# Later lead for the score pass and a later shift transpose in the forgetting-attention schedule

## The chip, the core and the metric

The kernel runs on one core of a Trainium2 chip. The metric is the device time in microseconds (us) of one launch. One launch computes both layers for 2048 tokens. Engines are named as in the profile: PE (TensorE), DVE (VectorE), ACT (ScalarE), POOL (GpSimd), SP (SyncE, which only issues transfers here).

## What is computed

The reference is two layers. Each normalises its input, projects it with one matrix, runs four groups of heads, gates them, projects back and adds the input. The change touches the first group alone, the forgetting attention: four heads of width 64, softmax over all earlier tokens with a decay that is added to the scores.

```python
def _fox_attention(q, k, v, f_logit, b_f, q_norm, k_norm):
    q = _rmsnorm(q, q_norm)
    k = _rmsnorm(k, k_norm)
    log_f = jax.nn.log_sigmoid((f_logit + b_f).astype(jnp.float32))
    Ft = jnp.cumsum(log_f, axis=1).transpose(0, 2, 1)
    ...
        s = jnp.einsum("bqhd,bkhd->bhqk", qi, k, preferred_element_type=jnp.float32) * scale
        s = s + Fi[..., :, None] - Ft[:, :, None, :]
        s = jnp.where(kpos[None, :] <= qpos[:, None], s, -jnp.inf)
        p = jax.nn.softmax(s, axis=-1)
        return jnp.einsum("bhqk,bkhd->bqhd", p.astype(v.dtype), v)
```

## The kernel before

Each layer is a row of phases, and every phase ends in a barrier of all engines. Their names are prefixes in the trace: pj, rp and rs (projection, recurrence), a normalising phase, fx (the forgetting attention, `phase_fox`), and so (the window attention, the short convolution, the output projection). What is won or lost inside fx moves everything behind it by the same amount, once in each layer.

In fx the work is cut into eight blocks, R = 0 to 7: two heads at a time (blocks 0 to 3 are heads 0 and 1, blocks 4 to 7 are heads 2 and 3), and for them four stretches of 512 queries. With Q = R % 4, a block has 4Q + 4 tiles of 128 keys. The softmax needs each query's greatest score before its exponentials, so each block is passed over twice. These are its steps, with the letter that the program's list `order` gives them:

- **r** (4 pieces): queries and keys of a block are rounded and their remainders taken (ACT, DVE, POOL). Pieces 2 and 3 cost DVE two operations each (L1321, L1322).
- **s** (4, 8, 12 or 16 pieces): first pass. PE makes scores with queries in the rows (L1244, and L1246 for the mask on the diagonal) into one of two PSUM buffers `SS`; DVE takes their greatest value (L1332). PE waits with piece n until DVE has done piece n - 2.
- **x**: DVE folds the greatest values of a block into `LS` (L1340), once all its s pieces are done.
- **l**: PE transposes `LS` into PSUM `LT` (L1253), ACT copies it into the block's query operand (L1390, two copies). The block's second pass cannot begin before it.
- **v**: PE transposes a block's values into the same `LT` (L1233), DVE copies them out (L1327). l, v and u (below) share the one `LT`, and each waits until the one before has been copied.
- **m** (4, 8, 12 or 16 tiles): second pass. PE makes the scores again with keys in the rows (L1268, L1269, L1271), ACT takes their exponential (L1407), PE multiplies the tile before by the values (L1223), and the exponentials are summed by DVE (L1311 for the first, L1314) or, for odd tiles outside Q = 0, by POOL (L1203, L1205). The last four tiles of a block are the diagonal ones, 512, 384, 256 and 128 queries wide.
- **o, u**: the block's result is copied out and divided by the sums.

Every engine runs its own part of the one list `order` strictly in the list's order. `plan()` writes that list: it walks through the m tiles, and after each one takes as many pieces of r, s, x and v (the list `beside`) as a running goal asks for. Two numbers matter here. The goal jumps up shortly before the end of a block, so that all s pieces of the next block are listed by then (L1123: from the fourth tile before the end). And l is put in turn by L1102: with the next block's turn less one tile, so in front of a block's last m tile, but never over four tiles behind x.

Of the kernel before, what the change touches and what calls it, by code (L numbers as in the profile page):

```python
# [1030 lines left out]
def phase_fox(nc, l, projT, fa, consts, mixT):  # L1031
# [6 lines left out]
    with ExitStack() as ctx:  # L1038
        P = Phase(nc, ctx, f"fx{l}")
        two = range(2)  # L1040
        NQ, QT = T // TB, TB // 128
# [13 lines left out]
        nm = [P.sb(f"nm{p}", [128, 2, NT, NQ]) for p in two]  # L1055
# [15 lines left out]
        keys = [QT * Q + QT for Q in range(NQ)]  # L1071
# [4 lines left out]
        def plan():  # L1076

            beside = [("r", 0, i) for i in range(4)] + [("v", 0, 0)]
            for R in range(NR):
                n = len(stat[R % NQ])
                for i in range(n):
                    if R + 1 < NR and i >= n - 4:
                        beside.append(("r", R + 1, i - n + 4))
                    beside.append(("s", R, i))
                beside.append(("x", R, 0))
                if R + 1 < NR:  # L1090
                    beside.append(("v", R + 1, 0))
            turns, order, done, ns, nm = [], [], 0, 0, 0
            total = sum(len(stat[R % NQ]) for R in range(NR))

            def ahead(goal):
                nonlocal done, ns
                while done < len(beside) and (ns < goal or beside[done][0] == "x"):
                    order.append(beside[done])
                    ns += beside[done][0] == "s"
                    if beside[done][0] == "x":  # L1100
                        r = beside[done][1]
                        turns.append((min(nm + 4, max(nm, sum(keys[i % NQ] for i in range(r)) - 1)), ("l", r, 0)))  # L1102
                    done += 1

            def turned(now):
                while turns and turns[0][0] <= now:
                    order.append(turns.pop(0)[1])

            ahead(len(stat[0]))
            turned(1)  # L1110
            ahead(len(stat[0]) + 3)
            for R in range(NR):
                for j in range(keys[R % NQ]):
                    turned(nm)
                    order.append(("m", R, j))
                    nm += 1
                    if R > 0 and j == 0:
                        order.append(("o", R - 1, 0))
                    if R > 0 and j == 2:
                        order.append(("u", R - 1, 0))  # L1120
                    goal = len(stat[0]) + 3 + min(nm, 24) * 3 // 2 + max(0, nm - 24) * 19 // 20
                    for r in range(1, NR):
                        if nm >= sum(keys[i % NQ] for i in range(r)) - 4:  # L1123
                            goal = max(goal, sum(len(stat[i % NQ]) for i in range(r + 1)))
                    ahead(min(total, goal))
            return order + [("o", NR - 1, 0), ("u", NR - 1, 0)]

        order = plan()
        lt_n = {}
        for k, R, x in order:  # L1130
# [786 lines left out]
```

## Time and profile before

| | |
|---|---|
| median of 3 runs | 3596.78 us (3592.81 to 3598.64) |
| the profiled execution's own time | 3596.78 us |
| its span | 3595.0 us |
| PE, PEld busy | 3230.6 us (90%), 2306.3 us |
| DVE, ACT, POOL busy | 1569.9 us, 1015.5 us, 546.7 us |
| fx in the first layer | about 1259 to 1540 us |
| fx in the second layer | about 3054 to 3336 us |

The page gives shares over the whole program. The change works in about 560 us of it, so the rows below are taken from the two fx stretches and read in order of time.

### The profile page before, as it was taken

Reading aid. Unit: us, or ns where it says so; the run is one execution under the profiler, and the core shown is the slowest. Engines: PE = TensorE matmul, PEld = TensorE weight load, DVE = VectorE, ACT = ScalarE, POOL = GpSimd, SP = SyncE. Lnnn points to the kernel's source line nnn. Section 1 sums busy time; section 2 is a strip of 40 time slices with the busy share of each in tenths; the row PEclk is TensorE's granted clock in tenths of the full one; section 3 lists DMA queues with packets and bytes.
Section 4 is the critical chain, followed back from the end, with each engine's and each line's share of the span. In section 5 each row is a group of like instructions: output and inputs, shape, how many; then the busy total and the mean of one; then the engine's idle time right before and its main releaser. Section 6 shows DMA issues by size and latency. Waiting matters only on the chain. (4 is left out here: it accounts for less than half of the span.)

```text
span 3595.0 us, 62105 instructions
## 1 busy us (share of the span) xinstructions
PE 3230.6 (90%) x24644; PEld 2306.3 (64%) x24644; DVE 1569.9 (44%) x2258; ACT 1015.5 (28%) x1892; POOL 546.7 (15%) x304
## 2 busy tenths in 40 slices
PE   6979979999998879959969799799999987799599
PEld 4768867777775244437748688577777752444377
DVE  4127722222223558557541277222222234675575
ACT  4014412122222135432240144121222221354322
POOL 4101000000000023332241010000000000233322
PEclk9989989999999769979989899899999996699799
DMA  3225432222222220067332254322222222100663
GB/s 121 73 72 160 144 95 63 66 66 69 77 67 99 118 58 27 9 195 214 117 116 73 72 169 138 93 66 63 66 73 75 66 106 109 58 27 9 194 214 117
DMA packets 357722, 343.27 MB, mean 95 GB/s; under 512 B 95388, under 2 KB 290972, under 8 KB 353592
## 3 DMA queue, kind: packets, MB, share of 16 engines
q1 hardware_dynamic: 288520, 298.53, 26.3%
q10 hardware_dynamic: 68928, 40.93, 4.2%
q8 instruction: 191, 3.13, 0.4%
q14 instruction: 83, 0.68, 0.1%
HBM read 208.46 MB, written 130.91 MB: 94 GB/s over the span
## 5 line engine op out<-in xcount | busy, mean ns | idle before, releaser
L124 PE MATMUL rs_acc<-h_hi,rs_w_hi 128*128 128x512 f32 x1024 | 428.3, 418 | 0.0
L128 PE MATMUL rs_acc<-h_lo,rs_w_hi 128*128 128x512 f32 x1024 | 417.8, 408 | 0.0
L130 PE MATMUL rs_acc<-h_hi,rs_w_lo 128*128 128x512 f32 x1024 | 414.5, 405 | 0.0
L110 POOL TENSOR_TENSOR rs_w_lo<-rs_raw,rs_w_hi 128x1024 fp32r<-128x1024 f32 x32 | 76.4, 2386 | 1236.2 <-POOLq L109 1236.2
L124 PE MATMUL rp_acc<-h_hi,rp_w_hi 128*128 128x512 f32 x512 | 205.5, 401 | 40.9 <-PEq L121 40.9
L1693 PE MATMUL so_acc<-so_wo_hi,so_m_hi 128*128 128x512 f32 x512 | 209.2, 409 | 27.7 <-POOL so_m_lo L1615 24.0
L124 PEld LDWEIGHTS rs_acc<-h_hi,rs_w_hi 128*128 128x128 f32 x1024 | 192.2, 188 | 55.0 <-issue 16.5
L130 PEld LDWEIGHTS rs_acc<-h_hi,rs_w_lo 128*128 128x128 f32 x1024 | 192.6, 188 | 43.2
L1407 ACT ACTIVATE fx_prob<-fx_ST 128x512 f32<-128x512 f32 (+3 forms) x320 | 155.5, 531 | 224.1 <-PE fx_ST L1271 129.7
L128 PEld LDWEIGHTS rs_acc<-h_lo,rs_w_hi 128*128 128x128 f32 x1024 | 192.7, 188 | 36.6
L124 PE MATMUL pj_acc<-h_hi,pj_w_hi 128*128 128x512 f32 (+1 forms) x512 | 207.6, 405 | 5.3 <-PEq L121 5.3
L141 ACT COPY rs_stage<-rs_acc 128x512 f32<-128x512 f32 x128 | 75.0, 586 | 483.3 <-ACTq L140 483.3
L128 PE MATMUL rp_acc<-h_lo,rp_w_hi 128*128 128x512 f32 x512 | 207.8, 406 | 0.0
L128 PE MATMUL pj_acc<-h_lo,pj_w_hi 128*128 128x512 f32 (+1 forms) x512 | 205.1, 401 | 0.0
L130 PE MATMUL pj_acc<-h_hi,pj_w_lo 128*128 128x512 f32 (+1 forms) x512 | 205.0, 400 | 0.0
L1695 PE MATMUL so_acc<-so_wo_lo,so_m_hi 128*128 128x512 f32 x512 | 204.6, 400 | 0.0
L1694 PE MATMUL so_acc<-so_wo_hi,so_m_lo 128*128 128x512 f32 x512 | 204.2, 399 | 0.0
L130 PE MATMUL rp_acc<-h_hi,rp_w_lo 128*128 128x512 f32 x512 | 200.4, 391 | 0.0
L1332 DVE TENSOR_REDUCE fx_nm<-fx_SS 128x2 f32<-128x1024 f32 (+3 forms) x160 | 166.9, 1062 | 34.3 <-PE fx_SS L1244 20.5
L141 DVE COPY pj_stage<-pj_acc 128x512 f32<-128x512 f32 (+1 forms) x64 | 44.2, 690 | 286.9 <-DVEq L140 286.9
L1223 PE MATMUL fx_O<-fx_prob,fx_vs 128*64 128x512 f32 (+3 forms) x640 | 161.5, 586 | 0.0
L1205 POOL TENSOR_TENSOR fx_sump<-fx_sump,fx_prob 128x1024 f32<-128x1024 f32 (+2 forms) x60 | 123.1, 2051 | 248.6 <-ACT fx_prob L1407 248.6
(256 smaller groups left out, 6055.7 us busy)
## 6 DMA issues: line engine op xcount, KB each, us to landing
projT<-rs_stage SPq DMA_DIRECT2D x128, 256.0 KB, 2.1
pj_xb<-x SPq DMA_DIRECT2D x32, 512.0 KB, 3.4
projT<-rp_stage SPq DMA_DIRECT2D x64, 256.0 KB, 3.1
rs_raw<-w_in ACTq DMA_DIRECT2D x32, 512.0 KB
rs_nat<-rw SPq DMA_DIRECT2D x128, 128.0 KB, 2.4
so_stage<-x SPq DMA_DIRECT2D x64, 256.0 KB, 3.0
rp_pre<-projT SPq DMA_DIRECT2D x16, 899.5 KB, 7.6
projT<-pj_stage SPq DMA_DIRECT2D x56, 256.0 KB, 2.0
```

Source lines behind the costliest of these rows:

```text
L110: self.nc.gpsimd.tensor_tensor(self.w_lo[q][:, :, 0:m], self.raw[:, :, 0:m], self.w_hi[q][:, :, 0:m].bitcast(F32), ALU.subtract).then_inc( ...
L124: ins = M(acc, self.w_hi[q][:, k, 0:m], self.h_hi[:, k, cols], start=(k == 0), stop=False)
L128: M(acc, self.w_hi[q][:, k, 0:m], self.h_lo[:, k, cols], start=False, stop=False)
L130: ins = M(acc, self.w_lo[q][:, k, 0:m], self.h_hi[:, k, cols], start=False, stop=(k == KC - 1))
L141: copy(self.stage[e][0:m, :], self.acc[e][0:m, :]).then_inc(self.stage_rdy[e], 1)
L1205: G.tensor_tensor(sump[R % 2][:, :, lo:TB], sump[R % 2][:, :, lo:TB], prob[nt % NP][:, :, lo:TB], ALU.add).then_inc(s["add_p"], 1)
L1223: ins = M(O[64 * h:64 * h + 64, lo:TB], vs[p][:, j, 64 * h:64 * h + 64], prob[i % NP][:, h, lo:TB], start=(j == 0), stop=(j == keys[Q] - 1))
L1332: V.tensor_reduce(nm[p][:, :, t, c:c + 1], SS[ns % 2][:, :, 0:width(t, c)], AX.X, ALU.max, negate=True).then_inc(s["m_rdy"], 1)
L1407: A(prob[nt % NP][:, h, lo:TB], ST[h][:, lo:TB], ACT.Exp).then_inc(s["p_rdy"], 1)
L1693: M(a, m_hi[e][:, c, rows], wo_hi[:, c, cols], start=(i == 0), stop=False)
L1694: M(a, m_lo[e][:, c, rows], wo_hi[:, c, cols], start=False, stop=False)
L1695: ins = M(a, m_hi[e][:, c, rows], wo_lo[:, c, cols], start=False, stop=(i == KC - 1))
```

## The change

Two numbers in `plan()` change, and nothing else.

```diff
-                        turns.append((min(nm + 4, max(nm, sum(keys[i % NQ] for i in range(r)) - 1)), ("l", r, 0)))
+                        turns.append((min(nm + 4, max(nm, sum(keys[i % NQ] for i in range(r)))), ("l", r, 0)))
...
-                        if nm >= sum(keys[i % NQ] for i in range(r)) - 4:
+                        if nm >= sum(keys[i % NQ] for i in range(r)) - 2:
```

The first puts l directly in front of the next block's first tile. The second lets the goal jump two m tiles later. Each engine's instructions stay the same in number and kind; their order changes at four places of each layer: the ends of blocks 0, 1, 2 and 6. At the ends of blocks 3, 4 and 5 the list stays as it was.

On PE at the end of block 1 (first layer), before the change, l (L1253) stands in front of the last m tile, and v (L1233) and an s piece (L1244) stand behind that tile:

```order
L1223 MATMUL fx_O<-fx_prob,fx_vs 64x384 x2
L1253 MATMUL fx_LT<-fx_ident,fx_LS 67x128 x4
L1268 MATMUL fx_ST<-fx_qa,fx_ka 128x128
L1269 MATMUL fx_ST<-fx_qb,fx_kb 128x128
L1271 MATMUL fx_ST<-fx_identb,fx_cmb 128x128
L1268 MATMUL fx_ST<-fx_qa,fx_ka 128x128
L1269 MATMUL fx_ST<-fx_qb,fx_kb 128x128
L1271 MATMUL fx_ST<-fx_identb,fx_cmb 128x128
L1223 MATMUL fx_O<-fx_prob,fx_vs 64x256 x2
L1233 MATMUL fx_LT<-fx_ident,fx_rv 128x128 x4
L1244 MATMUL fx_SS<-fx_kb,fx_qb 128x512 x2
L1268 MATMUL fx_ST<-fx_qa,fx_ka 128x512
```

In the changed kernel, at the same place on PE, from the last m tile's end:

```order
L1271 MATMUL fx_ST<-fx_identb,fx_cmb 128x128
L1223 MATMUL fx_O<-fx_prob,fx_vs 64x256 x2
L1233 MATMUL fx_LT<-fx_ident,fx_rv 128x128 x4
L1244 MATMUL fx_SS<-fx_kb,fx_qb 128x512 x2
L1253 MATMUL fx_LT<-fx_ident,fx_LS 67x128 x4
L1268 MATMUL fx_ST<-fx_qa,fx_ka 128x512
```

So l has moved behind the tile, behind v and behind the s piece, and the first matmul of block 2 follows it directly. Blocks 0 and 2 end in the same way; at the end of block 6 there is no v and no s piece left, and l moves over the last tile alone.

On DVE at the end of block 6, the difference is one sum (L1314, a tile of 512 queries and two heads) that moves from behind x (L1340) to between the last s pieces (L1332):

```order
 L1332 TENSOR_REDUCE fx_nm<-fx_SS 128x2 x2
 L1314 TENSOR_TENSOR fx_sumd<-fx_sumd,fx_prob 128x1024
-L1332 TENSOR_REDUCE fx_nm<-fx_SS 128x2 x4
+L1332 TENSOR_REDUCE fx_nm<-fx_SS 128x2 x2
+L1314 TENSOR_TENSOR fx_sumd<-fx_sumd,fx_prob 128x1024
+L1332 TENSOR_REDUCE fx_nm<-fx_SS 128x2 x2
 L1340 TENSOR_REDUCE fx_LS<-fx_nm 128x4 x2
-L1314 TENSOR_TENSOR fx_sumd<-fx_sumd,fx_prob 128x1024
```

On PE two m tiles have come forward between the s pieces there, and with them their exponentials on ACT and this sum on DVE. At the end of block 1 DVE's order changes in the same way:

```order
 L1332 TENSOR_REDUCE fx_nm<-fx_SS 128x2
 L1314 TENSOR_TENSOR fx_sumd<-fx_sumd,fx_prob 128x1024
-L1332 TENSOR_REDUCE fx_nm<-fx_SS 128x2 x5
+L1332 TENSOR_REDUCE fx_nm<-fx_SS 128x2 x3
+L1314 TENSOR_TENSOR fx_sumd<-fx_sumd,fx_prob 128x1024
+L1332 TENSOR_REDUCE fx_nm<-fx_SS 128x2 x2
 L1321 TENSOR_TENSOR fx_qa<-fx_rq,fx_qb 64x512
```

There the sum that followed x now stands three reductions after the sum before it, and two tiles of m have come forward on PE. At the end of block 2 two tiles come forward as well, and at the end of block 0 one.

## Rows read from the trace of the kernel before

**Rows 1.** Stretches of fx, layer one: us, busy PE PEld DVE ACT POOL, clock, DMA
```profile
1259.20:1540.00 280.80, 243.22 (x1048) 122.00 (x1048) 181.56 (x190) 127.05 (x249) 87.18 (x58) 0.88 0.10 31
...
1317.80:1334.80 17.00, 15.86 (x42) 7.38 (x44) 11.77 (x15) 2.56 (x5) 3.00 (x3) 0.50 0.11 33
...
1485.00:1495.30 10.30, 9.97 (x26) 4.26 (x26) 4.11 (x6) 2.18 (x4) 1.64 (x1) 0.50 0.00 0
```

**Rows 2.** Waits of PE from 1284 to 1540 us: total, times, longest
```profile
PE fx_SS L1244 <- DVE fx_nm L1332: 11.9, 13, 3.4
```

**Rows 3.** Timeline of PE, end of block 1: start, us, instruction [idle before]
```profile
1318.62 1.82 PE L1244 MATMUL fx_SS<-fx_kb,fx_qb 66*128 66x512 f32 x3 [2.37 <-DVE fx_nm L1332]
...
1325.05 0.78 PE L1268 MATMUL fx_ST<-fx_qa,fx_ka 128*128 128x512 f32 x1
...
1329.32 0.69 PE L1268 MATMUL fx_ST<-fx_qa,fx_ka 128*128 128x384 f32 x1
...
1338.51 0.40 PE L1268 MATMUL fx_ST<-fx_qa,fx_ka 128*128 128x512 f32 x1
```

**Rows 4.** Timeline of DVE, end of block 1
```profile
1317.89 1.81 DVE L1332 TENSOR_REDUCE fx_nm<-fx_SS 128x2 f32<-128x512 f32 x2
...
1328.82 0.24 DVE L1340 TENSOR_REDUCE fx_LS<-fx_nm 128x4 f32<-128x12 f32 x2
```

**Rows 5.** Groups of DVE by shape, layer one: count, busy us, mean ns, idle
```profile
L1314 DVE TENSOR_TENSOR fx_sumd<-fx_sumd,fx_prob 128x1024 f32<-128x1024 f32 x24 | 46.0, 1916 | 13.5 <-ACT fx_prob L1407 11.7 <-issue 0.2
...
L1327 DVE COPY fx_vs<-fx_LT 128x512 f32<-128x512 f32 x8 | 5.5, 688 | 8.6 <-PE fx_LT L1233 8.4
```

**Rows 6.** Timeline of PE, end of block 0
```profile
1294.64 0.67 PE L1268 MATMUL fx_ST<-fx_qa,fx_ka 128*128 128x384 f32 x1
...
1298.48 0.58 PE L1268 MATMUL fx_ST<-fx_qa,fx_ka 128*128 128x256 f32 x1
...
1301.13 0.65 PE L1253 MATMUL fx_LT<-fx_ident,fx_LS 128*67 128x128 f32 x4
...
1303.16 0.63 PE L1233 MATMUL fx_LT<-fx_ident,fx_rv 128*128 128x128 f32 x4 [0.24 <-ACT fx_qb L1390]
...
1304.10 0.40 PE L1268 MATMUL fx_ST<-fx_qa,fx_ka 128*128 128x512 f32 x1
```

**Rows 7.** Timeline of ACT, end of block 0
```profile
1301.82 1.19 ACT L1390 ACTIVATE fx_qb<-fx_LT 3x512 fp32r<-3x512 f32 x2 [1.33 <-PE fx_LT L1253]
```

**Rows 8.** Timeline of DVE, end of block 0
```profile
1291.07 2.17 DVE L1332 TENSOR_REDUCE fx_nm<-fx_SS 128x2 f32<-128x1024 f32 x2 [0.27 <-PE fx_SS L1244]
...
1298.41 0.23 DVE L1340 TENSOR_REDUCE fx_LS<-fx_nm 128x4 f32<-128x8 f32 x2
```

**Rows 9.** Timeline of PE, end of block 2
```profile
1364.65 0.73 PE L1244 MATMUL fx_SS<-fx_kb,fx_qb 66*128 66x512 f32 x2 [0.53 <-DVE fx_nm L1332]
...
1367.65 0.48 PE L1268 MATMUL fx_ST<-fx_qa,fx_ka 128*128 128x512 f32 x1
...
1369.97 0.44 PE L1268 MATMUL fx_ST<-fx_qa,fx_ka 128*128 128x384 f32 x1
...
1378.30 0.48 PE L1268 MATMUL fx_ST<-fx_qa,fx_ka 128*128 128x512 f32 x1
```

**Rows 10.** Timeline of DVE, end of block 6
```profile
1482.94 3.47 DVE L1332 TENSOR_REDUCE fx_nm<-fx_SS 128x2 f32<-128x1024 f32 x3
```

**Rows 11.** Timeline of PE, start of block 7
```profile
1499.22 0.47 PE L1268 MATMUL fx_ST<-fx_qa,fx_ka 128*128 128x512 f32 x1 [0.76 <-ACT fx_prob L1407]
```

**Rows 12.** Stretches of fx, layer two (columns of the first group)
```profile
3161.00:3167.80 6.80, 6.66 (x16) 2.73 (x16) 6.58 (x10) 1.44 (x3) 1.24 (x3) 0.50 0.04 8
...
3280.50:3290.70 10.20, 8.71 (x23) 3.97 (x24) 6.49 (x8) 1.69 (x3) 0.00 (x0) 0.50 0.00 0
```

**Rows 13.** Timeline of PE, layer two, end of block 2
```profile
3160.01 0.73 PE L1244 MATMUL fx_SS<-fx_kb,fx_qb 66*128 66x512 f32 x2 [0.53 <-DVE fx_nm L1332]
...
3176.00 0.48 PE L1268 MATMUL fx_ST<-fx_qa,fx_ka 128*128 128x512 f32 x1
```

## Prediction, made before the changed kernel ran

> **What bounds the kernel now.** I read the page first, then the stretches of fx with their granted clock, then PE's waits inside fx, then the timelines of PE, DVE and ACT at the ends of the four blocks whose order changes. Inside fx of the first layer PE is busy 243.2 of 280.8 us [rows 1], so fx is mostly PE-bound. What is left has three causes. The first is PE standing before an s piece for DVE's reductions, 11.9 us in 13 waits once the stage is under way, the longest 3.4 us [rows 2]. The second is the granted clock: it is 0.50 (1.2 GHz) over 17.0 us from the end of block 1 on, and over 10.3 us from the end of block 6 on, each time after a wait for DVE [rows 1, 3]. The third is at the start of fx and is not touched. The changed places are the ones with the longest waits, so the change works where something can be won, but on DVE and on the clock as much as on PE.
>
> What a tile costs at the two clocks: the 512-wide diagonal tile takes 1369.97 - 1367.65 = 2.32 us at 2.4 GHz at the end of block 2 [rows 9] and 1329.32 - 1325.05 = 4.27 us at 1.2 GHz at the end of block 1 [rows 3]. A microsecond of PE-bound work at the low clock thus wastes (4.27 - 2.32) / 4.27 = 0.46 us.
>
> **The change, place by place (first layer; the start of the next block's tiles before and after).** One chain is common to all: l starts at 1301.13, ACT's two copies run from 1301.82 to 1303.01, and PE gets the release at 1303.16 [rows 6, 7]. That is 2.0 us from the start of l to what waits for its copies. Before, this lay under the last m tile, v and an s piece. Now the next block's first matmul stands right behind l, and everything on PE is queued behind that matmul. PE itself does 0.6 us of the 2.0 and idles the rest. In front of l stands v's copy on DVE (0.69 us [rows 5]), since both use `LT`.
>
> End of block 0. One tile comes forward in front of four s pieces, at a moment when PE is the late one (DVE had idled only 0.27 us for the first of them [rows 8]). The tile takes 1298.48 - 1294.64 = 3.84 us at the low clock [rows 6], and DVE's whole row of reductions and remainders, unbroken up to x, is late by that: x ends at 1298.64 + 3.84 = 1302.5. Behind x DVE has two short sums that I take at 0.96 and 0.69 by their widths (384 and 256 queries, against 0.69 for the copy of as many elements as the second), then v's copy 0.69 and 0.15 for the release: l at 1305.0, block 1 at 1307.0. It was 1304.10 [rows 6]. Cost 2.9 us. If the remainders of block 2 absorb a part of it, the cost is 1.5.
>
> End of block 1. Before, PE stood 2.37 us for DVE [rows 3]; now a tile at full clock (2.3 us) fills just that. DVE is the chain from then on. From the end of its reductions at 1319.70 to the end of x at 1329.06 [rows 4] is 9.4 us, of which 0.5 was idle that goes; one sum is inserted. The 24 sums of that size take 1.92 us in the mean [rows 5], which I take; one that has DVE alone would be near the reductions of as many elements, 3.47 / 3 = 1.16 [rows 10]. So x ends at 1319.7 + 8.9 + 1.9 = 1330.5; then a sum of 0.69, v's copy 0.69 and 0.15: l at 1332.0, block 2 at 1334.0. It was 1338.51 [rows 3], since four tiles ran behind x at half clock. Gain 4.5 us (from 3.5 to 5.3 with the sum at 2.9 or 1.16).
>
> The Trainium skill, "GPSIMD Engine Reference", section Specifications, says that GpSimd shares its SBUF interfaces with VectorE, with contention for VectorE instructions that have two SBUF inputs, which these sums are. The trace agrees in the mean of 1.92 us against 1.16 for a reduction that reads PSUM [rows 5, 10]. By a rule of no contention the term would be 5.3 instead of 4.5.
>
> End of block 2. Here PE's waits were short (0.53 us and less) and the clock was full [rows 9], so the two tiles have little to fill. The second-last reductions now wait for PE (some 1.2 us), the sum adds 1.9, so x comes some 3.1 us later; the last m tiles, already done by then, don't help. With v, the small s pieces, l and its 2.0 us I get block 3 at about 1379.0 against 1378.30 [rows 9]. Cost 0.7, from -0.8 to 2.5.
>
> End of block 6. DVE's last four reductions began at 1482.94, the sum in front of them being done [rows 10]. Now: four reductions of 1.16, one sum of 1.92, 0.1 of latency and x 0.25 make 1489.85; l at 1490.0, block 7 at 1492.05. It was 1499.22 [rows 11]. Gain 7.2 us, from 6.0 to 8.0.
>
> Per layer at an unchanged clock from there: -4.5 - 7.2 + 2.9 + 0.7 = -8.1 us. The second layer has the same stage, so -16.2 us in both.
>
> **The clock takes it back.** The new waits sit close together. At the end of block 1 PE has done all its tiles by about 1329 and stands until 1332, does l, and stands again until 1334; at the end of block 6 it stands 1.1 and 1.4 us around l; at the end of block 0 some 1.5 and 1.4; at block 2 three short ones. Before, the clock fell after a single wait of 2.37 us [rows 3], and in the second layer it fell at the end of block 2 after waits of about 0.5 [rows 13]. So I expect falls at most of these places, and now just in front of the next block's tiles, which are PE-bound. Before, block 2's and block 7's first tiles ran at the full clock. The spans of 0.50 after a fall inside the stage are 6.8, 10.2 and 10.3 us [rows 1, 12], and 17.0 where PE was not dense. I take 8.5, less about 1 us that lies under the new wait: 7.5 x 0.46 = 3.4 us each. I take three falls of the four in each layer: 10.2 us. Per layer: -8.1 + 10.2 = +2.1 us, in both +4.2.
>
> One fall goes away. In the second layer the clock was low for 6.8 us at block 2 [rows 12], which the first layer did not have; between the same two matmuls, layer two took 3176.00 - 3160.01 = 15.99 us and layer one 1378.30 - 1364.65 = 13.65 [rows 9, 13]. So that fall cost 2.3 us, which is also the lower price of a fall. With the two tiles between the s pieces PE stays dense there: -2.3. Sum: +1.9 us. The profiled execution took 3596.78 us around its span of 3595.0, and the median of the runs is the same number, so the forecast is 3598.7 us. A measurement of this kernel can tell about 0.2% (7.2 us) from no change.
>
> Costed at nothing: the loads (SP's list is the same; their releases come some us later, far ahead of use), the casts of r on ACT and POOL (both idle half of the stage [rows 1]). If a load were late, PE would show a wait for a transfer, and does not now.
>
> **The rivals.**
> A, the clock holds. The tiles that come forward keep PE dense through the old waits, and the new waits are 1 to 1.5 us each with l between them. Then -16.2 - 2.3 is 3578, and with one fall in each layer 3585. For it: waits of 0.76 us in front of block 7 and 0.53 at block 2 passed at the full clock in layer one [rows 9, 11]. Against it: the wait of 2.37 [rows 3], and the new ones sum to more than that in as short a time. Chance 0.30.
> B, slower: the wait for l's copies, placed directly before a PE-bound stretch, sends the clock down at all four places and for the longer span. Its place is the first tiles of blocks 1, 2, 3 and 7, its price (10.2 - 1) x 0.46 = 4.2 us each, 16.9 a layer against the 8.1 gained: +8.8, in both +17.6, less 2.3: 3612. It decides from an average of 1.9 us a place on. With only three long falls it is 3603. Chance 0.25 for all four.
> C, the inserted sums cost DVE up to 2.9 us each and x is late everywhere: one more us at three places of each layer, +6, 3605. For it: the mean of 1.92 already holds doubled ones. Chance 0.10.
> The forecast, small gains and falls that cancel: 0.35, its own range 3590 to 3606.
>
> **Chances and range.** Faster by over 0.2%: A, nearly whole, and a little of the forecast, 0.31. Slower by over 0.2% (above 3604): B, half of C and a little of the forecast, 0.32. Within: 0.37. The range goes to the inner part of A and of B, 3582 to 3613.
>
> **What would show it.** In the profile after: PE's 2.37 and 3.4 us waits for the reductions at the ends of blocks 1 and 6 gone; one wait of 1 to 1.5 us on L1268 for ACT's copies L1390 in front of blocks 1, 2, 3 and 7, and none before; block 7's first tile about 9 us behind the start of the last four reductions instead of 16.3 [rows 10, 11]; fx_LT L1253 waiting for DVE (the copy of v, or x). And the granted clock: 0.50 just behind these waits if the forecast or B holds, 1.00 there if A does. The prediction is wrong if the clock stays up at three or more of the places, if block 0 does not start block 1 later, or if the time in fx changes by more than 9 us in a layer.

## The result and the profile after

The changed kernel takes 3625.73 us in the median of 6 runs (3617.81 to 3633.53), the kernel before 3597.71 us (6 runs, 3591.26 to 3603.74). The ratio is 1.0078 with a 95% interval of 1.0063 to 1.0093: 28 us slower. The forecast was 3598.7 and its range ended at 3613, so the prediction was wrong. The profiled execution has a span of 3622.8 us (before 3595.0) at a mean granted clock of 0.921 (before 0.929). The two stages of fx grew by 16.7 and 12.0 us, 28.7 together: all of the loss is there.

The page after, busy time of each engine. PE has the same 24644 matmuls and is busy 25.3 us longer (3230.6 before), so most of the loss is slower matmuls and not idle time (25.3 of the 27.8 us by which the span grew).

```profile
PE 3255.9 (90%) x24644; PEld 2321.5 (64%) x24644; DVE 1577.3 (44%) x2258; ACT 1018.9 (28%) x1892; POOL 549.4 (15%) x304
```

Stretches of fx in layer one, to be read beside [rows 1] (the third number from the end is the granted clock): the whole stage, then the part of block 1 that runs at half clock, the tiles from there to the next fall, and the low stretches at the starts of blocks 2, 3 and 7.

```profile
1259.20:1557.00 297.80, 259.05 (x1048) 130.93 (x1048) 185.47 (x190) 127.81 (x249) 87.57 (x56) 0.82 0.10 30
1307.20:1320.30 13.10, 13.07 (x34) 6.87 (x36) 3.48 (x4) 4.18 (x7) 1.04 (x1) 0.50 0.00 1
1320.30:1333.90 13.60, 12.16 (x53) 5.73 (x49) 11.07 (x10) 7.42 (x14) 6.09 (x4) 1.00 0.06 20
1333.90:1351.00 17.10, 15.46 (x50) 8.65 (x49) 9.87 (x13) 5.48 (x11) 2.00 (x3) 0.50 0.16 47
1385.00:1402.20 17.20, 14.89 (x40) 7.58 (x42) 8.52 (x16) 6.92 (x12) 1.31 (x2) 0.50 0.15 46
1508.00:1521.70 13.70, 12.55 (x30) 5.32 (x32) 0.69 (x1) 4.89 (x9) 1.04 (x1) 0.50 0.01 1
```

All four changed places run at half clock, for 13.1 to 17.2 us each. Before, there was one such stretch of 17.0 from the end of block 1 on and one of 10.3 from the end of block 6 on [rows 1]; the low clock from the start of fx ended at 1300.7, ahead of block 1 (1304.10). Now that first low clock goes on 13.1 us into block 1, and PE is busy 13.07 of these 13.10 us, so it does dense work at half clock the whole time. In layer two the clock rises for 3.4 us near the end of block 0 and falls again for 17.1 us, of which 6.7 lie in block 1; the stretches of blocks 2, 3 and 7 there are 17.1, 17.1 and 13.7 us.

Waits of PE in layer one after the change, to be read beside [rows 2]: total, times, longest.

```profile
PE fx_SS L1244 <- DVE fx_nm L1332: 8.5, 13, 1.9
PE fx_ST L1268 <- ACTq L1392: 6.5, 4, 1.6
PE fx_LT L1253 <- DVE fx_LS L1340: 1.1, 1, 1.1
```

The waits for DVE's reductions fell from 11.9 to 8.5 us, and the longest from 3.4 to 1.9. In their place stand four waits for ACT's copies of `LT` (L1392 is the release behind L1390) and one for x (L1340). The three rows sum to 16.1 us against 11.9, but over the whole program PE's idle time grew by only 27.8 - 25.3 = 2.5 us.

Timeline of PE in layer one: the first matmul of block 1, the tile that came forward at the end of block 1, the first matmuls of blocks 2 and 3, then l and the first matmul of block 7. To be read beside [rows 3, 6, 9, 11].

```profile
1307.23 0.77 PE L1268 MATMUL fx_ST<-fx_qa,fx_ka 128*128 128x512 f32 x1 [1.62 <-ACTq L1392]
...
1325.18 0.39 PE L1268 MATMUL fx_ST<-fx_qa,fx_ka 128*128 128x512 f32 x1
...
1344.22 0.77 PE L1268 MATMUL fx_ST<-fx_qa,fx_ka 128*128 128x512 f32 x1 [1.62 <-ACTq L1392]
...
1390.73 0.77 PE L1268 MATMUL fx_ST<-fx_qa,fx_ka 128*128 128x512 f32 x1 [1.62 <-ACTq L1392]
...
1506.85 0.65 PE L1253 MATMUL fx_LT<-fx_ident,fx_LS 128*67 128x128 f32 x4 [1.06 <-DVE fx_LS L1340]
...
1509.15 0.77 PE L1268 MATMUL fx_ST<-fx_qa,fx_ka 128*128 128x512 f32 x1 [1.65 <-ACTq L1392]
```

The first matmul of blocks 2, 3 and 7 took 0.40, 0.48 and 0.47 us before and takes 0.77 now. The wait is 1.62 us at three of the places and 1.65 at the fourth.

Timeline of DVE in layer one: at the end of block 1 an inserted sum, at the end of block 2 the inserted sum, a remainder behind it and x, then the end of block 6.

```profile
1330.02 1.23 DVE L1314 TENSOR_TENSOR fx_sumd<-fx_sumd,fx_prob 128x1024 f32<-128x1024 f32 x1
...
1377.05 1.22 DVE L1314 TENSOR_TENSOR fx_sumd<-fx_sumd,fx_prob 128x1024 f32<-128x1024 f32 x1
1378.19 2.32 DVE L1321 TENSOR_TENSOR fx_qa<-fx_rq,fx_qb 64x512 fp32r<-64x512 f32 x1
...
1385.40 0.25 DVE L1340 TENSOR_REDUCE fx_LS<-fx_nm 128x4 f32<-128x16 f32 x2
...
1499.48 2.34 DVE L1332 TENSOR_REDUCE fx_nm<-fx_SS 128x2 f32<-128x1024 f32 x2
1501.92 2.26 DVE L1314 TENSOR_TENSOR fx_sumd<-fx_sumd,fx_prob 128x1024 f32<-128x1024 f32 x1
```

Two of the inserted sums took 1.23 and 1.22 us and one 2.26. The remainder behind the sum of block 2 took 2.32 us, where most others of its kind in this stage took 0.67 to 0.69.

### The profile page after: what moved, and what is told of

It is laid out like the page before. It is cut to its first block and busy times, and to the rows that moved or that the text cites. A ratio compares the mean times of both kernels' runs of the same rounds, so it can differ in the third digit from the quotient of the medians.

```text
span 3622.8 us, 62105 instructions
## 1 busy us (share of the span) xinstructions
PE 3255.9 (90%) x24644; PEld 2321.5 (64%) x24644; DVE 1577.3 (44%) x2258; ACT 1018.9 (28%) x1892; POOL 549.4 (15%) x304
## 5 line engine op out<-in xcount | busy, mean ns | idle before, releaser
L1332 DVE TENSOR_REDUCE fx_nm<-fx_SS 128x2 f32<-128x1024 f32 (+3 forms) x160 | 166.5, 1061 | 70.3 <-PE fx_SS L1244 51.5
L1223 PE MATMUL fx_O<-fx_prob,fx_vs 128*64 128x512 f32 (+3 forms) x640 | 170.7, 617 | 0.0
```

Of the source, the lines that this page charges most:

```text
L1223: ins = M(O[64 * h:64 * h + 64, lo:TB], vs[p][:, j, 64 * h:64 * h + 64], prob[i % NP][:, h, lo:TB], start=(j == 0), stop=(j == keys[Q] - 1))
L1332: V.tensor_reduce(nm[p][:, :, t, c:c + 1], SS[ns % 2][:, :, 0:width(t, c)], AX.X, ALU.max, negate=True).then_inc(s["m_rdy"], 1)
```

## The experiments

The expectations name four theories by letters. The first two ask which half of the change costs: the wait behind l (W), where the later l alone costs and the later goal gains, or the goal (G), where the later goal costs, through DVE's sums. The other two ask by what it costs: the clock (C), where the waits of the new order keep PE at 1.2 GHz and the loss goes if PE is given something to do in them, or the waits and DVE's later work themselves (D), where the clock only goes along and filling the waits changes nothing. "Before" in each comparison is the kernel before in the same session (medians 3595.2, 3597.98 and 3596.48).

**One half of the change at a time.** The later l alone (L1102) and the later goal alone (L1123):

```diff
-  turns.append((min(nm + 4, max(nm, sum(keys[i % NQ] for i in range(r)) - 1)), ("l", r, 0)))
+  turns.append((min(nm + 4, max(nm, sum(keys[i % NQ] for i in range(r)))), ("l", r, 0)))
```
```diff
-  if nm >= sum(keys[i % NQ] for i in range(r)) - 4:
+  if nm >= sum(keys[i % NQ] for i in range(r)) - 2:
```

> Theory W (the move of l alone does the harm: a wait of 1.6 us for ACT's two copies in front of blocks 1, 2, 3 and 7, and a fall of the granted clock with it): at least 20 of the 28 us of the whole change show here, 3616 to 3635 us, with four waits of L1268 for L1392 in each layer, and more low clock in fx than before. Theory G (the goal's move does it, by sums of 1.2 to 2.4 us put into DVE's row before x, and by the tile that comes forward at block 0): under 10 us over the kernel before, below 3608.

Measured: 3638.04 us, ratio 1.0111 (1.0086 to 1.0136).

> Theory W: with l where it was, the moved goal is a gain: the waits of 2.4 and 3.4 us at blocks 1 and 6 are filled, block 0 costs about 2, so 3583 to 3596 us. Theory G: most of the 28 us is here, 3615 or more, with x later at blocks 0, 1 and 2.

Measured: 3618.71 us, ratio 1.0062 (1.0044 to 1.0079). Each half costs by itself, 43 and 23 us, and both together cost 28. W asked for a gain of the later goal and G for a later l that costs under 10, so neither holds; and the 3638 us lie above W's range. The waits of PE in layer one of the later l alone:

```profile
PE fx_SS L1244 <- DVE fx_nm L1332: 10.6, 11, 3.4
PE fx_ST L1268 <- ACTq L1392: 6.8, 4, 1.9
```

And of the later goal alone, with its low stretches around the starts of blocks 2 and 3 (columns of the stretches above):

```profile
PE fx_SS L1244 <- DVE fx_nm L1332: 7.4, 11, 1.9
PE fx_LT L1253 <- DVE fx_LS L1340: 5.4, 3, 2.4
PE fx_LT L1253 <- DVE fx_vs L1327: 2.9, 1, 2.9
```
```profile
1332.20:1356.10 23.90, 21.95 (x68) 12.37 (x69) 11.54 (x15) 6.56 (x13) 2.82 (x4) 0.50 0.11 33
1386.80:1407.30 20.50, 19.37 (x58) 9.73 (x58) 8.35 (x16) 7.97 (x15) 1.76 (x2) 0.50 0.14 39
```

The later l brings the four waits for ACT and leaves the 3.4 us wait; the later goal takes that one away and makes l wait for x and v instead. Either way the clock is low for 106 to 107 us in layer one (before 61).

**Something for PE to do in the waits.** The following kernels issue extra matmuls in front of chosen instructions. They write a score buffer that the next tile overwrites, so they change no output. The list `FILL` says where and how many: `("m",1,0): 7` is 7 matmuls in front of tile 0 of block 1. The `wait_ge` holds them until that buffer is free. Here it is for the changed kernel, 48 in each layer.

```diff
+            def keep_busy(n):
+                if n:
+                    pe.wait_ge(s["p_rdy"], 2 * nt - 1)
+                for _ in range(n):
+                    M(ST[0][:], K1[0][0][:, 0:128], Q1[0][0][:, 0:TB], start=True, stop=True)
+            FILL = {("m",1,0): 7, ("m",2,0): 7, ("m",3,0): 7, ("m",7,0): 7, ("l",7,0): 4,
+                    ("s",2,10): 2, ("s",2,11): 2, ("s",4,0): 8, ("s",4,1): 3, ("s",4,2): 1}
...
+                    keep_busy(FILL.get((k, R, x), 0))   # ahead of s, l and m
```

> The changed kernel, with matmuls of no use (each 128x512, 0.23 us at 2.4 GHz) put on PE where it waits at the four places: 7 in front of the first tile of blocks 1, 2, 3 and 7, 4 in front of l of block 7, 12 among the s pieces of block 4 and 4 among those of block 2. They write a score buffer that the next tile overwrites. Theory C (most of the loss is the granted clock at 1.2 GHz behind the waits): the low stretches behind the four places vanish or shrink, and the time falls by 12 to 30 us below the changed kernel's 3625, to 3596 to 3613, though PE has more to do. Theory D (the loss is the waits and DVE's later row, the clock only goes along): the time stays, or grows by up to 10 us, since nothing waits less.

Measured: 3591.6 us, ratio 0.9989 (0.9979 to 0.9999). With 96 matmuls more than the changed kernel it is 34 us faster than it, more than theory C had expected (3596 to 3613), and D is out. Its stretches in layer one: the stage, its one low stretch behind block 0, and all behind that.

```profile
1263.20:1530.70 267.50, 248.68 (x1096) 130.31 (x1096) 181.10 (x187) 124.42 (x246) 80.70 (x52) 0.91 0.09 27
1332.00:1338.80 6.80, 5.53 (x15) 4.22 (x15) 2.35 (x3) 1.66 (x3) 0.00 (x0) 0.50 0.32 101
1338.80:1530.70 191.90, 186.28 (x861) 92.78 (x860) 132.50 (x127) 94.80 (x189) 68.55 (x40) 1.00 0.05 17
```

The same for the kernel before, filled at its own waits (s pieces of blocks 2, 3 and 7, 36 in each layer):

```diff
+            FILL = {("s",2,7): 10, ("s",2,9): 1, ("s",2,10): 1, ("s",2,11): 2,
+                    ("s",7,14): 14, ("s",7,15): 2, ("s",3,13): 2, ("s",3,14): 2, ("s",3,15): 2}
```

> The kernel before, with the same kind of matmul put under its own waits for the reductions: 14 among the s pieces 7 to 11 of block 2, 6 among s pieces 13 to 15 of block 3, 16 in front of s pieces 14 and 15 of block 7. Theory C: the low stretches of 17.1 us behind block 1 and 10.2 us behind block 6 go, and with them 0.46 us for each us that PE was dense in them, 4 to 5 and 4 us in each layer, and 2 in the second layer at block 2: 3575 to 3585 us. Theory D: no gain, 3592 to 3605.

Measured: 3575.39 us, ratio 0.9945 (0.9928 to 0.9961). So the kernel before loses up to 20 us of this kind as well (the two stages of fx show 15 of them in the profiled executions), and the clock does not hide a gain of the change: filled against filled, it still costs 16 us.

**The control.** The same number of matmuls in the kernel before, put where PE does not wait:

```diff
+            FILL = {("m",3,4): 9, ("m",3,6): 9, ("m",3,8): 9, ("m",3,10): 9}
```

> A control: the kernel before, with 9 of the matmuls of no use in front of each of the tiles 4, 6, 8 and 10 of block 3, where PE is dense and the clock full, so 36 in a layer as many as before_busy has. If the matmuls gain by something other than filled waits, this is no slower. By their own length, 72 x 0.235 us, it is 17 us slower: 3608 to 3616.

Measured: 3610.32 us, ratio 1.0033 (1.0022 to 1.0043). So 72 matmuls cost 12 us where PE is busy and bring 20 where it waits; it is their place that counts. Layer one of the control beside that of the filled kernel before:

```profile
1266.90:1544.50 277.60, 253.00 (x1084) 129.23 (x1084) 177.04 (x187) 124.62 (x246) 80.01 (x52) 0.88 0.09 26
```
```profile
1266.40:1528.40 262.00, 243.59 (x1084) 125.53 (x1084) 178.41 (x187) 124.17 (x246) 79.31 (x52) 0.92 0.09 28
```

**Which waits decide.** The changed kernel with 7 matmuls in front of the first tile of blocks 1, 2, 3 and 7 and nothing else, and then with only the others of its list:

```diff
+            FILL = {("m",1,0): 7, ("m",2,0): 7, ("m",3,0): 7, ("m",7,0): 7}
```
```diff
+            FILL = {("l",7,0): 4, ("s",2,10): 2, ("s",2,11): 2, ("s",4,0): 8, ("s",4,1): 3, ("s",4,2): 1}
```

> The changed kernel with 7 matmuls of no use in front of the first tile of blocks 1, 2, 3 and 7 alone, so only the new waits of 1.6 us are filled and not those among the s pieces and in front of l. If these four waits are what brings the clock down, the time is that of after_busy, 3591 us, up to 3600. If the waits before them (1.85 and 0.7 us at block 3, 1.1 us at block 7, the thin s pieces at block 2) are enough, the low stretches of blocks 2, 3 and 7 stay, only block 1's goes, and the time is 3608 to 3622.

Measured: 3592.84 us, ratio 0.9981 (0.997 to 0.9991).

> The complement of after_m_busy: the changed kernel with the matmuls of no use among the s pieces of blocks 2 and 4 and in front of l of block 7, but none in the four new waits of 1.6 us. If those four waits are what brings or keeps the clock down, this stays near the changed kernel, 3612 to 3628 us. If either half of the filling is enough, it is 3592 to 3605.

Measured: 3609.72 us, ratio 1.0039 (1.0024 to 1.0054), between the two expectations. The waits and stretches of the first of the two:

```profile
PE fx_SS L1253 <- DVE fx_nm L1343: 8.5, 13, 1.9
PE fx_LT L1263 <- DVE fx_vs L1338: 3.2, 1, 3.2
PE fx_LT L1263 <- DVE fx_LS L1351: 1.1, 1, 1.1
```
```profile
1303.00:1306.80 3.80, 3.78 (x14) 2.82 (x13) 2.41 (x4) 1.09 (x2) 0.00 (x0) 0.52 0.46 135
1306.80:1333.90 27.10, 24.35 (x117) 12.82 (x115) 20.05 (x19) 12.43 (x26) 8.65 (x6) 1.00 0.03 11
1334.10:1340.90 6.80, 5.07 (x14) 4.20 (x15) 2.72 (x5) 1.20 (x3) 0.00 (x0) 0.51 0.39 116
1378.40:1385.20 6.80, 6.43 (x20) 4.93 (x21) 4.72 (x9) 2.33 (x4) 0.00 (x0) 0.50 0.39 114
```

This is the sharpest of the runs. Before the s pieces PE waits for DVE just as in the changed kernel, 8.5 us in 13 waits, and at the ends of blocks 1 and 2 the clock falls there too. But the low stretches last 6.8 us instead of 17.1 and 17.2, the low clock at the start of block 1 ends at 1306.8 instead of 1320.3, and the stretch at block 7 is gone. 33 of the 34 us come back with the four waits of 1.62 us. The clean comparison is block 3, where both kernels have the same waits in front (1.85 and 0.71 us) and fall at the second of them: 17.2 us low with the wait behind l open and 6.8 with it filled (in layer two 17.1 and 10.2, though there the filled kernel falls already at the first of the two). At block 2 they are not alike: block 1 now runs at full clock, PE is done sooner and stands 3.2 us for the copy of v (the second row above), a wait that the changed kernel doesn't have, and the clock falls inside it. So at blocks 2 and 3 the wait behind l doesn't bring the fall; at block 3 it prolongs it, at block 2 that is likely but not isolated. At block 7 there is no fall any more, so there the wait behind l did bring it. In the second kernel, where the four waits are left, the low stretches at blocks 2 and 3 last 10.2 and 13.7 us:

```profile
1335.90:1346.10 10.20, 8.13 (x22) 4.34 (x22) 3.36 (x4) 4.16 (x7) 0.72 (x1) 0.50 0.17 54
1383.70:1397.40 13.70, 12.65 (x32) 5.77 (x34) 5.15 (x9) 4.82 (x9) 1.04 (x1) 0.50 0.05 16
```

**The halves again, with the waits filled.** The later l with the kernel before's list and 7 in front of the four first tiles; the later goal with its own list:

```diff
+            FILL = {("l",1,0): 4, ("s",2,10): 2, ("s",2,11): 2, ("l",2,0): 8,
+                    ("s",4,0): 8, ("l",3,0): 10, ("l",7,0): 10}   # later goal
```

> Only l is moved, and the matmuls of no use lie under the waits: those of the run before_busy, and 7 in front of the first tile of blocks 1, 2, 3 and 7. Against before_busy (3575 us) this gives the price of l's move at an unfallen clock. Theory C: four waits of 1.6 to 2.0 us a layer, less what PE's earlier waits for LT gave, so 8 to 16 us: 3583 to 3592, against the 43 us that the move cost with the clock free to fall. Theory D: 3605 or more.

Measured: 3585.53 us, ratio 0.9957 (0.9944 to 0.997).

> Only the goal is moved, with the matmuls of no use under its waits: 4, 8, 10 and 10 in front of l of blocks 1, 2, 3 and 7, 8 among the s pieces of block 4 and 4 among those of block 2. Theory C: the 23 us that the move cost turn into a gain against the kernel before, 3570 to 3588 us, but it needn't beat before_busy (3575). If the fall comes from the s pieces themselves, some low clock stays behind block 1 and the time is 3588 to 3600. Theory D: 3615 or more.

Measured: 3586.09 us, ratio 0.9971 (0.9958 to 0.9984), with single runs from 3575.5 to 3596.88. Against the filled kernel before (3575.4) the halves cost 10 and 11 us and both together 16, by the medians of two sessions; by the ratios to the kernel before of each session it is 4, 9 and 16, and the intervals of the two halves overlap with that of the filled kernel before. The profiled executions tell more. Their two stages of fx take 523.8 us in the filled kernel before, 530.2 with the later l, 522.2 with the later goal and 535.0 with both. So at a mostly kept clock the later l costs 6 us there. That the later goal costs is not shown: in fx it takes 1.6 us less, and its single executions follow their granted clock (3575.5 us at 0.939, 3596.88 at 0.931), which suggests that its filling holds the clock in some executions better than in others.

**A version that beats both.** By the segments (next section) the later goal pays in front of blocks 2 and 7 only. So it is kept there, without the later l, with its waits filled:

```diff
-  if nm >= sum(keys[i % NQ] for i in range(r)) - 4:
+  if nm >= sum(keys[i % NQ] for i in range(r)) - (2 if r in (2, 7) else 4):
+            FILL = {("s",2,10): 2, ("s",2,11): 2, ("l",2,0): 8, ("l",7,0): 10,
+                    ("s",3,13): 2, ("s",3,14): 2, ("s",3,15): 2}
```

> The kernel before with the moved goal for blocks 2 and 7 only (where the kernel before waited 2.4 and 3.4 us), l where it was, and the matmuls of no use in what waits remain. From the times of the blocks in the traces of goal_busy and before_busy: 2.4 us less between the starts of blocks 1 and 2, and 1.9 less between 6 and 7, in each layer: 3564 to 3571 against 3575 of before_busy. If the two gains exist only through the clock, it is the same as before_busy.

Measured: 3573.64 us, ratio 0.9943 (0.9927 to 0.996), no better than the filled kernel before that can be told. The expected gain is in the trace: the two stages of fx take 514.7 us against 523.8. But that execution is the fastest of four, which reach up to 3579.22. Then the start of fx, which runs at half clock in every kernel so far: 20 matmuls with the identity as soon as its constants have arrived (the trace counts two instructions for each), and 30 more between the first s pieces and at l and v; once on the filled kernel before, once on the last version. The second line stands for entries that are added to the list:

```diff
+            for _ in range(20): M(ST[0][:, 0:128], ident[:], ident[:], start=True, stop=True)
...
+            FILL = {..., ("s",0,0): 5, ("s",0,2): 9, ("l",0,0): 10, ("v",1,0): 4, ("s",1,2): 2}
```

> before_busy, and PE kept busy through the start of fx as well, where the clock is low for 51 us up to the end of block 0: 20 matmuls of 128 columns on the unit matrix while POOL prepares, and 30 in the waits of block 0's first pass. If the clock then comes up before block 0's tiles begin, the 14 us of dense work up to 1301 us cost about 6 less in each layer: 3560 to 3568 us. If 128-column matmuls are too thin to bring it up, no change: 3572 to 3580.

Measured: 3573.81 us, ratio 0.9939 (0.9922 to 0.9955).

> mix_busy and before_warm together, the version to beat the kernel before with: the two gains add if they touch different blocks, 3550 to 3562 us; 3564 to 3575 if only one of them is real.

Measured: 3569.56 us, ratio 0.9935 (0.9912 to 0.9958): the fastest version, 27 us under the kernel before, though its interval overlaps those of the other three. Both missed the gain that was hoped for and landed where their expectations had put "no change" and "only one of them is real", though for the first not for the reason given there, since the clock does rise. Timeline of PE at the start of fx and stretches of the first of the two:

```profile
1265.76 7.68 PE L1213 MATMUL fx_ST<-fx_ident 128*128 128x128 f32 x40 [12.03 <-DMA fx_cm<-consts]
1273.28 0.60 PE L1248 MATMUL fx_LT<-fx_ident,fx_rv 128*128 128x128 f32 x4
```
```profile
1271.40:1289.10 17.70, 13.97 (x111) 12.50 (x110) 11.76 (x18) 7.75 (x14) 3.52 (x6) 0.98 0.40 117
1289.10:1302.80 13.70, 13.59 (x40) 7.45 (x39) 10.52 (x15) 5.79 (x11) 0.00 (x0) 0.50 0.07 22
...
3058.80:3309.90 251.10, 237.95 (x1146) 125.20 (x1144) 179.84 (x187) 121.67 (x242) 78.57 (x50) 0.99 0.09 28
```

The clock does rise early, but the constants arrive only at 1265.76, so v of block 0 now stands behind 7.68 us of matmuls and starts at 1273.28, some 7 us later than in the filled kernel before, and in layer one the clock falls again for 13.7 us. In layer two it stays at 0.99, and the stage takes 251.1 us there. What tells the two layers apart I did not find out.

## Why the prediction was wrong, point by point

The time of each segment on PE, between the starts of the first instruction (v) of block 0, the first tiles of the blocks and the end of fx, in us, layer one. All are differences of starts in the timelines.

```
                    blk 0  blk 1  blk 2  blk 3  4 to 6  blk 7    sum   at 0.50
before               36.7   34.4   39.8   45.5    75.5   36.8  268.7      60.7
after                40.9   37.0   46.5   49.5    68.9   42.5  285.4     101.7
after, filled        41.9   32.1   43.2   44.4    68.8   37.1  267.5      48.3
before, filled       37.3   31.5   39.8   45.5    71.0   36.8  262.0      41.5
later l, filled      38.9   33.7   41.1   44.4    72.0   36.8  267.0      40.2
later goal, filled   38.4   29.2   41.9   45.5    69.1   37.1  261.2      34.9
```

In layer two the sums are 269.9, 281.9, 267.5, 261.9, 263.2 and 261.0 us, and at 0.50 stand 67.4, 91.4, 48.3, 41.5, 31.2 and 33.3.

The forecast for fx was -16.2 (both layers, at an unchanged clock) - 2.3 (a fall that goes away) + 20.4 (three falls a layer) = +1.9 us. Measured by the table it is -3.6 (first to third line, both layers) + 32.3 (third to second line) = +28.7. Two terms failed, the price of the clock by 11.9 us and the gain of the new order by 14.9. The split is good to a few us: the third line still has one low stretch of 6.8 us in each layer, and its 7 matmuls at half clock in front of block 1 overrun the wait that they fill, so its block 0 is 1.0 us longer than in the second line (1.6 in layer two).

- "I take three falls of the four in each layer", 3.4 us each, 10.2 a layer. This is the first step that failed. The clock was low at all four places, for 13.1, 17.1, 17.2 and 13.7 us in layer one, not 8.5. The difference of the second and third line prices it: -1.0 + 4.9 + 3.3 + 5.1 + 0.1 + 5.4 = 17.8 us in layer one (17.9 unrounded) and 14.4 in layer two, 32.3 against the 20.4 (2 x 10.2) of the sum. The time at 0.50 differs by 96.5 us between the two kernels, so a microsecond at the low clock cost 0.33 us, less than the 0.46 I took; the number and length of the stretches were off by more than that. I had set the 17.0 us stretch aside as one "where PE was not dense", though its row has PE busy 15.86 of 17.00 us [rows 1].
- "Per layer at an unchanged clock from there: -8.1 us." This is the second step that failed, and the larger one. Predicted were +2.9, -4.5, +0.7, -7.2. From the first to the third line it is +5.2, -2.3, +3.4, -1.1, -6.7 and +0.3: -1.2 in layer one and -2.4 in layer two. Block 6 was right: its waits were filled with tiles, and block 7 starts 1509.15 - 1499.48 = 9.67 us behind the start of the last four reductions, for which I had said 9. In layer one blocks 0 and 2 cost 2.3 and 2.7 us more than I gave them, and block 1 gained half.
- Why even that gain is none: the fourth line. If the kernel before keeps its clock it wins 2.9 us at block 1 and 4.5 at blocks 4 to 6, the very places where the change gains. A large part of my mechanical gain was tiles no longer running at half clock. Against the filled kernel before the change costs +4.6, +0.6, +3.4, -1.1, -2.2 and +0.3 us, 5.5 in layer one. The two layers give 11 of the 16 us between the medians (13 between the two profiled executions).
- At block 0 I saw no fall to price, since the clock was low there anyway. But before, it rose in front of block 1; after, it rose 13.1 us into it. x itself came 3.6 us later behind v, near the 3.84 that I had; v, the s piece and l in front of block 1 now run at half clock (l takes 1.09 us, 0.65 before).
- At block 2 DVE's row shows what was missing. From the first of the last reductions to the end of x it took 8.8 us before (1363.63 to 1372.39) and takes 13.2 now (1372.42 to 1385.65): a wait for PE of 1.22, the sum of 1.22, and the two remainders behind it 2.32 + 1.00 instead of 0.79 + 0.69. So x came 4.5 us later and not 3.1. It is 13.2 us in the filled kernel too, so this is not the clock. DVE's rows there, before and then after:

```profile
1363.63 3.22 DVE L1332 TENSOR_REDUCE fx_nm<-fx_SS 128x2 f32<-128x768 f32 x3 [0.16 <-PE fx_SS L1246]
1366.77 0.79 DVE L1321 TENSOR_TENSOR fx_qa<-fx_rq,fx_qb 64x512 fp32r<-64x512 f32 x1
1367.57 0.69 DVE L1322 TENSOR_TENSOR fx_ka<-fx_rk,fx_kb 64x512 fp32r<-64x512 f32 x1
```
```profile
1372.42 2.09 DVE L1332 TENSOR_REDUCE fx_nm<-fx_SS 128x2 f32<-128x768 f32 x2 [0.16 <-PE fx_SS L1246]
...
1380.52 1.00 DVE L1322 TENSOR_TENSOR fx_ka<-fx_rk,fx_kb 64x512 fp32r<-64x512 f32 x1
```

- "One fall goes away" in layer two, -2.3 us: it did not. That place has a low stretch in both layers now.
- The waits themselves came as written: the 2.37 and 3.4 us ones gone, one of 1.62 us (I had 1 to 1.5) before each of the four blocks, and one of L1253 for x. Of the signs of being wrong that I had named, one came: fx changed by 16.7 and 12.0 us a layer, over the 9.
- Rival A is out: the clock was low at every place. Rival B named the right mechanism, all four places and, in sum, the right price: 2 x 16.9 = 33.8 us against the 32.3. That is in part luck, since its stretches were too short (9.2 us net, where 96.5 / 8 = 12.1 were added) and its rate too high (0.46 against 0.33). Its 3612 was too low because it kept the gain of 16.2 + 2.3 us, of which 3.6 came.
- Rival C took up to 2.9 us for each inserted sum. The sums took 1.23, 1.22 and 2.26. With the remainders behind them, block 1 has 1.9 us in all, as forecast, block 2 has 3.1 and block 6 has 2.3. So C's price holds at block 2 alone, and in another instruction than the sum.

The two halves separate the cost at a mostly kept clock, in layer one against the filled kernel before: the later l costs 1.6, 2.2 and 1.3 us at blocks 0, 1 and 2, gains 1.1 at block 3 and costs 1.0 at blocks 4 to 6 (in layer two, where it has no low stretch of 6.8 us, block 1 gains 0.6); the later goal costs 1.1 and 2.1 us at blocks 0 and 2 and gains 2.3 and 1.9 at block 1 and blocks 4 to 6, a part of the 2.3 through the clock, since the kernel before has a low stretch of 6.8 us there. What stays open: why the gains of the goal shrink when both are made together, and why the granted clock of one and the same filled kernel differs between executions.

## What to carry to other kernels

A wait that is moved from under other work to directly in front of a PE-bound stretch must be priced twice: its own length, and what is lost while the clock stays low behind it. Before crediting a reordering with the time of a wait it removes, ask whether that wait's cost was the wait or the half clock behind it, since a few throw-away matmuls in the wait buy the second part without any reordering (here 20 us by the medians). And price the gain of a new order against the old order at the same clock. And when a fall already happens in front of the place, look at what decides when the clock rises again, not at whether it falls.

## What the runs showed of the hardware

- At block 3 a wait of 1.62 us in a low stretch prolonged it from 6.8 to 17.2 us (from 10.2 to 17.1 in layer two), though PE was busy 14.89 of these 17.20 us. Filling four waits of this length in each layer, 13 us in all, took 33 us back.
- At the start of block 1 of the changed kernel the granted clock stayed at 0.50 for 13.10 us in which PE was busy 13.07.
- The fall at the end of block 1 comes at 1333.9, 7.6 us ahead of l: behind waits of only 0.27, 0.23, 0.55 and 0.40 us on L1244, none of them near the 2.37 behind which it had fallen before [rows 3].
- In layer one of the changed kernel, the low stretches at the start of blocks 2 and 3 lasted 6.8 us with the four waits behind l filled, 10.2 and 13.7 with the others filled, and 17.1 and 17.2 with none. In layer two it was 3.4 and 10.2, 10.2 and 13.7, and 17.1 and 17.1.
- An extra 128x512 matmul where PE is busy costs 0.23 us: block 3 of the control takes 1433.82 - 1380.17 = 53.65 us, before 1423.76 - 1378.30 = 45.46, for 36 of them. And 36 of them in the waits of a layer save 268.7 - 262.0 = 6.7 us in layer one and 8.0 in layer two.
- The two element-wise kinds on DVE vary with what POOL does beside them. In the kernels before and after, both layers, all 17 sums of 128x1024 that no POOL instruction of fx overlaps took 1.22 or 1.23 us, and the 79 that one overlaps took 1.22 to 3.29; of the remainders of L1321 the 42 without an overlap took 0.67 or 0.68, and the one of 2.32 had 2.17 us of it. The 224 reductions of 128x1024, which read PSUM, took 1.21 to 1.23 us, overlapped or not. An overlap is not enough to slow a sum: the one at 1330.02 took 1.23 us with POOL busy beside it. The Trainium skill, "GPSIMD Engine Reference", section Specifications, says that GpSimd shares its SBUF interfaces with VectorE, with contention for VectorE instructions that have two SBUF inputs, which fits these numbers; no run took POOL's work away to isolate it.
